# Token rows of the first expert pass by one-hot product instead of row list and gather, in a two-layer diffusion backbone with mixtures of experts

## The reference

```
scores = sigmoid(h @ router_w)
biased = scores + router_b
group  = argmax over 4 groups of (sum of the top 2 biased scores in it)
idx    = top 2 experts inside that group
w      = scores[idx] / sum(scores[idx])
for e in range(16):
    u   = silu(h @ w_gate[e]) * (h @ w_up[e])
    out = out + combine[:, e] * (u @ w_down[e])
x = x + gate * out
```

## Time and profile before

| | |
|---|---|
| median of 3 runs | 1349.01 us (1345.36 to 1351.83) |
| the profiled execution | 1346.76 us |
| its span in the trace | 1345.1 us |
| mean granted clock of TensorE | 0.974 |
| busy: TensorE, VectorE, ScalarE, GpSimd | 93%, 40%, 28%, 15% |
| DMA over the span | 352.31 MB, 262 GB/s |

### The profile page before, as it was taken

How to read it: one execution, slowest core, us unless ns; L and a number is a source line. 1 busy time by engine, 2 the same in 40 slices (tenths; PEclk the granted TensorE clock), 3 DMA queues, 4 the chain that set the end, 5 groups by cost and what they waited for, 6 DMA issues and landing times.

```text
span 1345.1 us, 14790 instructions
## 1 busy us (share of the span) xinstructions
PE 1253.1 (93%) x5911; PEld 585.6 (44%) x5911; DVE 542.0 (40%) x890; ACT 371.9 (28%) x712; POOL 205.3 (15%) x197
## 2 busy tenths in 40 slices
PE   5899999999999999979999998899999899988677
PEld 3344444444444444573333442444445474332212
DVE  1457466575656222562111111753419473121003
ACT  2335657566675300110000000310227211000000
POOL 1001334344343300010000002111101200000001
PEclk9999999999999999989999998999999979999889
DMA  9233665767556653378999999940000687999996
GB/s 360 98 129 125 219 216 192 252 242 258 205 203 232 218 210 140 151 289 343 426 427 427 429 427 420 390 147 0 1 16 1 263 335 308 426 428 428 428 428 242
DMA packets 76078, 352.31 MB, mean 262 GB/s; under 512 B 9337, under 2 KB 27433, under 8 KB 60641
## 3 DMA queue, kind: packets, MB, share of 16 engines
q1 hardware_dynamic: 67643, 326.16, 61.5%
q10 hardware_dynamic: 5132, 13.58, 2.6%
q0 software_dynamic: 3232, 11.59, 2.3%
HBM read 338.99 MB, written 12.33 MB: 261 GB/s over the span
## 4 chain that ended last, share of the span: by engine, by line
PE 74%; DMA 13%; DVE 7%; ACT 2%; SPq 1%; issue 1%; ACTq 1%; POOL 0%; POOLq 0%; DVEq 0%
PE psum L1695 20%; PE psum L2379 10%; PE psum L771 10%; PE psum L782 8%; PE psum L1116 6%; DMA ring<-in_moe_w_down 4%; DMA ring<-in_moe_w_up 4%; PE psum L299 3%; PE psum L2431 2%; PE psum L815 2%; PE psum L835 1%; DMA moe_y_d<-arena 1%; PE psum L1753 1%; DMA arena<-mod_d 1%; PE psum L831 1%; PE psum L259 1%
## 5 line engine op out<-in xcount | busy, mean ns | idle before, releaser
L1695 PE MATMUL psum<-ring,arena 128*32 128x512 f32 (+2 forms) x1568 | 348.4, 620 | 30.2 <-DMA ring<-in_moe_w_gate 11.6
L1695 PEld LDWEIGHTS psum<-ring,arena 128*32 128x32 f32 (+2 forms) x1568 | 103.2, 126 | 217.8 <-issue 170.8
L771 PE MATMUL psum<-hT,ring 128*128 128x512 f32 x384 | 169.7, 596 | 0.0
L2379 PE MATMUL psum<-ring,hT 128*128 128x512 f32 x320 | 139.7, 595 | 0.0
L1116 PE MATMUL psum<-ring 128*128 128x512 f32 x256 | 113.8, 602 | 2.1 <-ACT ring L930 1.3
L782 PE MATMUL psum<-hT,ring 128*128 128x512 f32 x256 | 112.5, 592 | 0.0
L771 PEld LDWEIGHTS psum<-hT,ring 128*128 128x128 f32 x384 | 71.3, 190 | 91.3 <-issue 91.3
L1695 PE MATMUL psum<-hT,arena 128*64 128x512 f32 (+2 forms) x208 | 92.7, 642 | 5.4 <-DMA hT<-in_moe_w_down 3.8
L976 DVE SCALAR_TENSOR_TENSOR arena<-arena,cols 128x512 f32<-128x512 f32 x96 | 92.7, 965 | 3.4
L2379 PEld LDWEIGHTS psum<-ring,hT 128*128 128x128 f32 x320 | 60.5, 191 | 73.5 <-issue 72.8
L1695 PE MATMUL psum<-arena 128*32 128x512 f32 (+2 forms) x288 | 80.1, 610 | 0.0
(11 more groups left out here) (353 smaller groups left out, 1562.3 us busy)
## 6 DMA issues: line engine op xcount, KB each, us to landing
ring<-in_moe_w_up SPq DMA_DIRECT2D x26, 2048.0 KB, 20.8
ring<-in_moe_w_gate SPq DMA_DIRECT2D x25, 2048.0 KB, 15.9
ring<-in_moe_w_down SPq DMA_DIRECT2D x22, 2048.0 KB, 21.5
arena<-in_ada_w SPq DMA_DIRECT2D x60, 512.0 KB, 5.9
ring<-in_ssd_w_in SPq DMA_DIRECT2D x16, 1024.0 KB, 7.1
ring<-acs_d SPq DMA_DIRECT2D x16, 1024.0 KB, 7.0
hT<-in_moe_w_down SPq DMA_DIRECT2D x6, 2048.0 KB, 19.9
ring<-in_da_w_in SPq DMA_DIRECT2D x6, 2048.0 KB, 19.0
```

What stands on the lines that cost most here:

```text
L771: mm = pe.matmul(psum[:, bank, :], w_[:, k, c0:c0 + P], hT[:, k, :], start=(k == 0), stop=(k == KD - 1))
L1695: mm = pe.matmul(psum[rows, dst, :], lhsT[:, k, rows], slot(s_, a)[:, k, part], start=(k == 0), stop=(k == a - 1))
L2379: mm = pe.matmul(psum[:, 4 + m_ % 2, :], hT[:, k, t * P:(t + 1) * P], slot(qkv_slot[n], KD)[:, k, :], start=(k == 0), stop=(k == KD - 1))
```

## The change

In moe0, group 0 gets its tokens in the way that moe1 uses. The four finished row tiles are kept in SBUF (`arena` columns 4096 to 8191, which is slot 6), the middle result and the norm's gain row move to columns 10240 and 11264. The row list, its cast and the gather of group 0 go; the rows are still stored, for the gathers of groups 1 to 9. TensorE forms the tokens of group 0 by 32 products, four tiles accumulated for each of eight blocks. The load of slot 6 also waits for these products. In both mixtures the mask of group 0 is made by one compare: each of the two experts is compared only with its own 64 columns, so that the result is already the sum over the two. The keep-busy products change: 18 instead of 10 behind the last logits in both mixtures, and 10 behind the rank products, instead of 12 in moe1 and of 15 and 20 in moe0.

```diff
-                self.h = h if isinstance(h, list) else [h[:, n, :] for n in range(h.shape[1])]
+                self.h = h
                 self.whole = int(g is not None)
+                if self.whole:
+                    self.rows, self.mid = h[:-1], h[-1]
...
-                act.dma_start(self.h_d[n * P:(n + 1) * P, :], self.h[n % 2]).then_inc(self.stored[n % 2], 16)
+                act.dma_start(self.h_d[n * P:(n + 1) * P, :], self.rows[n]).then_inc(self.stored[n % 2], 16)
...
                 v.wait_ge(self.s["rst"], self.at["rst"] + n + 1)
-                if n >= 2:
-                    v.wait_ge(self.stored[n % 2], self.stored_at[n % 2] + 16 * (n // 2))
...
             moe0.logits_part(pe, 2)
-            keep_busy(pe, 4, 10)
+            keep_busy(pe, 4, 18)
...
-        ngb, nh, njunk = carve(arena, 4096, D), carve(arena, 5120, 3, D), carve(arena, 8192, D)
+        ngb, njunk = carve(arena, 11264, D), carve(arena, 8192, D)
+        nh = [carve(arena, 4096 + n * D, D) for n in range(TT)] + [carve(arena, 10240, D)]
...
-                self.first = G * (nt < TT)
+                self.masked = nt < TT
+                self.first = G if self.masked else 1
+                self.mask0 = carve(arena, 8704, nt, P)
...
-                if self.first:
-                    keep_busy(pe, 5, 12)
-                    return
-                keep_busy(pe, 5, 15)
-                pe.wait_ge(*self.routed("FIRST"))
-                for t in range(nt):
-                    for e in range(2):
-                        m = pe.matmul(psum[:, 7, 0:1], self.onehot_0[:, 2 * t + e, :], self.tokf[:, t:t + 1],
-                                      start=(t + e == 0), stop=(t == nt - 1 and e == 1))
-                m.then_inc(s["rank_mm"], 1)
-                keep_busy(pe, 5, 20)
+                keep_busy(pe, 5, 10)
...
-                sv = self.sv.rearrange("p t e -> p (t e)")
-                if self.first:
-                    step(tt(out=first2[0], in0=self.many(self.iota128, 2 * nt), in1=over(sv, P), op=ALU.is_equal))
-                    tt(out=first1[0], in0=first2[0][:, 0:2 * nt:2, :], in1=first2[0][:, 1:2 * nt:2, :], op=ALU.add).then_inc(s["route_done"], 1)
-                else:
-                    tt(out=self.onehot_0, in0=self.many(self.iota128, 2 * nt), in1=over(sv, P), op=ALU.is_equal).then_inc(s["route_done"], 1)
+                halves_ = self.iota128.rearrange("p (o e c) -> p o e c", o=1, e=2).broadcast_to([P, nt, 2, P // 2])
+                tt(out=self.mask0.rearrange("p t (e c) -> p t e c", e=2), in0=halves_, in1=expand(self.sv, P // 2), op=ALU.is_equal).then_inc(s["route_done"], 1)
...
-                if not self.first:
-                    v.wait_ge(s["rank_mm"], at["rank_mm"] + 2)
-                    v.tensor_copy(self.idx[:, 0:1], psum[:, 7, 0:1]).then_inc(s["route_done"], 1)
...
                     pool.wait_ge(self.row_stored[j], self.at["rows"][j] + 16 * (nt // 2))
-                if not self.first:
-                    pool.wait_ge(*self.routed("IDX0"))
...
-                        m = pe.matmul(psum[:, k // 4, (k % 4) * P:(k % 4 + 1) * P], self.norm.h[t][:, k * P:(k + 1) * P], first1[j][:, t, :],
+                        m = pe.matmul(psum[:, k // 4, (k % 4) * P:(k % 4 + 1) * P], self.norm.rows[t][:, k * P:(k + 1) * P], (first1[j] if n else self.mask0)[:, t, :],
...
             moe1.logits_part(pe, 1)
-            keep_busy(pe, 5, 10)
+            keep_busy(pe, 5, 18)
...
-            moe0.sync_first(sp, SLOTS, ([moe0.scored()], stored))
+            moe0.sync_first(sp, SLOTS, ([moe0.scored()], stored + [(moe0.s["h_T_mm"], 2)]))
```

More of the change, by code:

```diff
@@ L475, in tile_mid @@
                 v.wait_ge(self.src_ready[n][0], self.src_ready[n][1])
-                step(v.tensor_tensor(out=self.h[2], in0=self.src[:, self.tiles[n], :], in1=self.A[:, cd - self.conds[0], :], op=ALU.mult))
+                step(v.tensor_tensor(out=self.mid, in0=self.src[:, self.tiles[n], :], in1=self.A[:, cd - self.conds[0], :], op=ALU.mult))
             def tile_out(self, v, n):
@@ L482, in tile_out @@
                 v.wait_ge(self.s["rst"], self.at["rst"] + n + 1)
-                if n >= 2:
-                    v.wait_ge(self.stored[n % 2], self.stored_at[n % 2] + 16 * (n // 2))
                 by_k = "p (q k) -> p q k"
-                v.scalar_tensor_tensor(out=self.h[n % 2].rearrange("p (k q) -> p q k", k=KD), in0=self.h[2].rearrange(by_k, k=KD),
+                v.scalar_tensor_tensor(out=self.rows[n].rearrange("p (k q) -> p q k", k=KD), in0=self.mid.rearrange(by_k, k=KD),
                                        scalar=rstd[:, t:t + 1], in1=self.S[:, cd - self.conds[0], :].rearrange(by_k, k=KD),
@@ L1241, in __init__ @@
                 G = self.ng = len(order)
-                self.first = G * (nt < TT)
-                done = (["M", "FIRST", "IDX0", "AB", "PERM", "IDX", "POS", "LAST"] if not self.first else
+                self.masked = nt < TT
+                self.first = G if self.masked else 1
+                self.mask0 = carve(arena, 8704, nt, P)
+                done = (["M", "FIRST", "AB", "PERM", "IDX", "POS", "LAST"] if not self.masked else
                         ["M", "FIRST", "MASK1", "PERM", "POS", "MASK2", "LAST"] + [f"MASK{n}" for n in range(3, G)])
@@ L1303, in __init__ @@
                 counts = dict(router_in=self.in_all, shifted=len(self.parts), table_zeroed=16, logits_mm=len(self.parts), sig=len(self.parts), pool_const=4, consts=2,
-                              route_done=len(done), rank_mm=4 if not self.first else 2, last_ready=1 + (nt == 4), last_mm=2 * nt, summed=2 * (nt == 4), h_T_mm=2 * G, hgT_a=G, hgT_b=G, gate_mm=G, silu=G,
+                              route_done=len(done), rank_mm=2 if self.masked else 3, last_ready=1 + (nt == 4), last_mm=2 * nt, summed=2 * (nt == 4), h_T_mm=2 * G, hgT_a=G, hgT_b=G, gate_mm=G, silu=G,
                               up_mm=G, u_ready=G, uT_mm=G, uT_ready=G, down_mm=G, ya=G, yb=G, gates_in=16 * len(self.conds), combined=nt)
@@ L1362, in __init__ @@
                 self.rwA, self.rwS, self.rwR, self.c_row = kt(nc_, KD, NE), kt(nc_, KD, NE), kt(nc_, NE), kt(nc_, NE)
-                self.onehot_s, self.onehot_0 = carve(arena, 14336, 2 * nt, P), carve(arena, 15360, 2 * nt, P)
+                self.onehot_s = carve(arena, 14336, 2 * nt, P)
                 self.grid, self.hit = carve(arena, 0, NE, NE), carve(arena, 256, NE, NE)
@@ L1587, in place_vector @@
                 step(stt(out=self.slotv, in0=self.grpv, scalar=-float(P), in1=self.rowv, op0=ALU.mult, op1=ALU.add))
-                if self.first:
+                if self.masked:
                     self.tokens_mask(v, step, 1)
@@ L1600, in place_vector @@
                 v.tensor_copy(self.perm, self.permf).then_inc(s["route_done"], 1)
-                if not self.first:
-                    v.wait_ge(s["rank_mm"], at["rank_mm"] + 3)
+                if not self.masked:
+                    v.wait_ge(s["rank_mm"], at["rank_mm"] + 2)
                     v.tensor_copy(self.idx[:, 1:G], psum[:, 7, 129:128 + G]).then_inc(s["route_done"], 1)
@@ L1855, in scalar @@
                     if n == 1:
-                        act.wait_ge(s["rank_mm"], at["rank_mm"] + (2 if self.first else 4))
+                        act.wait_ge(s["rank_mm"], at["rank_mm"] + (2 if self.masked else 3))
                         act.activation(MT[:, 0:self.nt, :], psum[:, 7, 0:self.nt * P].rearrange("p (t c) -> p t c", t=self.nt),
```

## The result

The changed kernel took 1333.53 us (median of 4 runs, 1330.74 to 1337.17) against 1347.61 us before, a ratio of 0.9895 (95% interval 0.9869 to 0.9922). Timed again with the experiments (label e5_after) it took 1336.38 us (6 runs) against 1348.06 us, ratio 0.9903 (0.9880 to 0.9926). The median of all ten of its runs is 1335.9 us. So it is 12 to 14 us faster; forecast were 9.6 us, and the first median lies at the lower edge of the range. The profiled execution took 1335.75 us (span 1334.0), 11.0 us less than that of before, although its rank products happened to start 1.7 us later; counted from there to its end it is 12.8 us shorter (749.3 against 762.1 us).

A forecast was written before the change was run, and what follows sets the result against it. TensorE's serial routing path in moe0 up to the first slot release was taken to bound the kernel; -9.8 + 0.75 - 0.5 = -9.6 us gave 1339.4 us against the median of 1349.01, range 1333.5 to 1345.5.

The forecast's parts named there:

- the term of moe1: Routing of moe1: keep-busy changes bring the token product forward, taken as -0.5 us, bounds -3.0 and +1.0.
- No slack behind the first release: Behind 612.1 in moe0 TensorE and the weight stream run without slack, so an earlier release moves the whole stage.
- Keep-busy in front, moe0: Before moe0's rank products: 18 calls take 4.46 us, hidden by 0.4 us before VectorE's last count.
- Mask, token product, index products: moe0 routing: mask compare 0.69 us, 32 token products 7.14 us, index products 1.8 us; TensorE last by 1 us.
- Release in moe0: Group 0's gate products end at 602.3 instead of 612.1, releasing the first slots 9.8 us earlier.
- The gather of group 1: In moe0, needed at 602.3, lands at 603.05: a wait of 0.75 us, bounds 0 and 4.3 us.
- the bound of -3.0: Best case for moe1: all keep-busy products run at 2.4 GHz, -3.0 us instead of -0.5.
- The moved load: moe0: slot 6's load waits for the token product, 593.6 instead of 589.87; nobody else is held.
- The term of moe0: moe0: group 0's gate products end 9.8 us earlier without row list, cast, gather and transposes.
- The bytes bind: Rival: the weight stream's unchanged bytes set the end whatever TensorE does; no gain, 1349 us; chance 0.10.
- The halved clock throughout: Rival, moe0: keep-busy through gate products run at 1.2 GHz throughout; +13 us, 1362 us; chance 0.06.
- A clock already low in front of the rank products of moe0: Rival: clock low at 579.8, token product 2.8 us later; with a late gather 1345.7 us; chance 0.16.

The follow-up runs named there:

- e5_after, e5: The changed kernel unaltered, timed again with the experiments: 1336.38 us, ratio 0.9903 to before.
- e6: The kernel before with only moe1's three edits (18 and 10 keep-busy products, mask in one compare), moe0 as it was: 1346.68 us, ratio 0.9984 to before.
- e3: The kernel before with 18 instead of 10 keep-busy products behind the last logits in both mixtures, nothing else: 1347.44 us, ratio 0.9990 to before.
- e4: The changed kernel with 30 instead of 10 keep-busy products behind the rank products of moe0: 1338.19 us, ratio 0.9928 to before.
- e8: The changed kernel with 6 instead of 10 keep-busy products behind the rank products in both mixtures: 1335.60 us, ratio 0.9893 to before.
- e10: The kernel before with the load of slot 6 behind the gather of group 0 and moe1 as changed: 1337.92 us, ratio 0.9910 to before.
- e11: The changed kernel with 6 instead of 10 keep-busy products behind the rank products in both mixtures, a second time: 1335.04 us, ratio 0.9900 to before.
- e12: The changed kernel with 6 instead of 10 keep-busy products behind the rank products in moe1 only: 1333.69 us, ratio 0.9887 to before.
- e7: The kernel before with slot 6 loaded only after the gather of group 0 has landed: 1339.43 us, ratio 0.9941 to before.
- e9: The kernel before with 36 instead of 20 keep-busy products behind the row list of moe0: 1344.83 us, ratio 0.9974 to before.
- e1: The changed kernel with 10 instead of 18 keep-busy products behind the last logits in both mixtures: 1336.67 us, ratio 0.9915 to before.
- e2: The changed kernel with moe1 as it was before, moe0 as changed: 1335.20 us, ratio 0.9910 to before.

## Why the prediction fell short

The direction and the path were right, the size was too small: 9.6 us against 12.2, which is what the distances add up to (10.1 in moe0, 2.1 in moe1). By time it is 12.6 us between the medians of all runs (1348.5 and 1335.9 us), and 14.1 in the first comparison. The step that failed is the term of moe1. Of the 2.6 us between 9.6 and 12.2 it has 1.6; 0.3 are moe0's, and 0.75 were entered for a late gather that no stretch shows as lost.

- **No slack behind the first release.** Right for the stream: every kernel has 195.6 to 196.4 us of it behind the release.
- **Keep-busy in front, moe0.** Forecast 4.46 us, hidden by 0.4; measured 4.26 us and 0.62 us of idle time.
- **Mask, token product, index products.** Forecast 0.69, 7.14 and 1.8 us; measured 0.69, 7.31 and 1.85 in the timeline (7.15 and 1.70 in the chain, from whose rows they were forecast). TensorE, not the mask, is last, by 0.8 us.
- **Release in moe0.** Forecast 9.8 us earlier; measured 10.1 in both profiles of the changed kernel. The gate products took 7.09 us at the full clock, with TensorE busy all the way from the rank products. The Trainium skill (TensorE: Matmul & The Clock Gate, Part 1, "What's actually happening") has the halved clock as the default that activity lifts; this trace agrees.
- **The gather of group 1.** Forecast a wait of 0.75 us; measured 0.59, and the gather took 6.47 us from issue to the transposes. Whether it cost anything is not shown: in the two profiles of the changed kernel the stream was 0.9 and 0.4 us longer than in that of before, but it was 0.8 us longer in e6 too, where nothing waits for this gather.
- **moe1: this step failed.** The prediction took from one profile that the clock falls before the last count, so that the eight extra products would run at 1.2 GHz, end 2.2 us late and leave -0.5 us. (Its own working, 1104.9 against 1105.75, gives -0.85; the -0.5 is stated without a reason for the rest.) In all executions with 18 products in moe1 (changed, e3, e4, e5, e6, e8, e10, e11, e12) they ran at 2.4 GHz, the idle time shrank from 2.35 to about 0.6 us, and the clock did not fall between them and the release. The term measured -2.1 us against the usual 16.04 us, and -3.6 us between the two profiles. The case of the bound of -3.0, everything at 2.4 GHz, is what happened; by the rows that bound should have been -3.4 (1098.98 + 1.0 + 2.4 against 1105.75).
- **The moved load.** The prediction entered the later load of slot 6 as a cost to be checked and found it hidden, which was right: nothing on TensorE waits for slot 6 in the profile of the changed kernel. It did not see that on the kernel before that same move is worth 8.0 us by itself. It had read the 7.25 us as those of a gather "beside one slot load", and did not ask what the gather takes without it. Nor did it see that the last row store landed within 1.1 us of the row list. The term of moe0 came out right in spite of it, because the change takes gather and collision away together: e7's 7.2 us of distance and the token product's further 3.0 make the 10.1.
- **Rivals.** "The bytes bind" doesn't fit e4, and e7 refutes it: the same bytes, 8.0 us less. The halved clock throughout did not occur. A clock already low in front of the rank products of moe0 was not seen in any profile with 18 products there. A drop further on was, in e8 and e11, for 1.5 us.

What stays open: how often the clock holds on the path through the gather. e10 has 12.1 us by its ratio beside a distance of 26.53 us, so its profiled execution can hardly be a typical one, and e9, meant to take the clock alone, kept half of the drop.

## What to carry to other kernels

Before an operation is replaced because its transfer is slow, look at what else was issued in the same few microseconds: a 2 MB prefetch that nobody needed soon, sent just ahead of a small transfer on the critical path, made that transfer 2.7 to 4.4 us longer here, and one wait on the prefetch gave back 8.0 of the 12 to 14 us of the redesign. A wait of TensorE can have two prices, its length and the halved clock behind it; cover it with work up to the expected end, and check the cover over several executions, since the one in the profile may be the exception. And measure a stage by a distance between two events of it, which here repeated to 0.01 us for the path without idle time, where whole runs spread by several; on the path through the gather it did not repeat (22.19 and 26.53 us).

## What the runs showed of the hardware

- The gather of 128 rows of 4 KB took 4.5 us from issue to the transposes that waited for it where no load was issued just ahead of it (e7, e10), and 7.2 to 8.9 us when a load of 2 MB was issued 0.8 to 2.0 us ahead of it (7.3 in before, 7.2 in e6, 8.4 in e3, 8.9 in e9).
- A row store of 512 KB, issued 0.4 us behind a load of 2 MB and 5 to 7 us behind two more, landed 11.1 or 11.2 us later, and the gather that needs it was held until then in e3, e7 and e9.
- Idle times of 2.34 to 2.42 us between keep-busy products and rank products were followed by about 3.5 us at 1.2 GHz in four of four places in moe1 (e1, e2, e7, e9) and in three of six in moe0 (before, e6, e10, and not e1, e7, e9). Idle times of 0.55 to 0.65 us were not followed by it in any of 17. In moe1 such a drop cost 1.6 us.
- 32 products of 128 columns, four tiles accumulated for each block, took 7.15 us in the chain, 0.22 us each, as did the 16 two-tile products in moe1 (3.57 us).
